# A decoder layer on one core: the output projection and the MLP with channels on the partitions, the token factor moved behind the squared ReLU

## The reference, cut to what matters

```python
merged = gates[:, :, 0] * y_attn + gates[:, :, 1] * y_pool
x = x + merged @ w_o                                  # output projection, 1024 x 1024
h2 = x * rsqrt(mean(x * x, -1) + EPS) * norm2_g       # pre-norm of the MLP, per token
u = square(relu(h2 @ w_mlp_in))                       # 1024 x 4096
x = x + u @ w_mlp_out                                 # 4096 x 1024
```

## Time and profile before

| | before |
|---|---|
| median of the runs | 1241.32 us (1241.32 to 1242.48) |
| the profiled execution | 1241.36 us, span 1239.5 us |
| PE busy | 1228.6 us, 99% of the span |
| DVE busy | 945.4 us, 76% |
| ACT busy | 563.9 us, 45% |
| POOL busy | 139.2 us, 11% |
| output projection, first matmul | 531.6 us |
| last output tile ends (the last `add_res` starts) | 625.3 us |
| down product begins (the last `up_add` of pair 15 starts) | 932.2 us |
| last matmul ends (the last add starts) | 1236.9 us |

### The profile page before, as it was taken

One profiled execution on the slowest core, in us unless ns is written; L12 is line 12 of the kernel. 1 busy time (PEld: TensorE's weight loads), 2 busy tenths in 40 slices (PEclk: granted clock), 3 DMA queues, 4 the chain that ended last, 5 costly groups with the idle time before them and its releaser, 6 DMA issues.

```text
span 1239.5 us, 16100 instructions
## 1 busy us (share of the span) xinstructions
PE 1228.6 (99%) x5822; PEld 1014.1 (82%) x5822; DVE 945.4 (76%) x1334; ACT 563.9 (45%) x971; POOL 139.2 (11%) x188
## 2 busy tenths in 40 slices
PE   8999999999999999999999999999999999999999
PEld 6878888887878888888888888888888888888887
DVE  6857876788887597845678867777769988879764
ACT  7546666665644323312345544535545333333330
POOL 1122233224100040000000000000000000000035
PEclk9999999999999999999999999999999999999999
DMA  9201211023564556422214354353479544262223
GB/s 368 78 17 35 64 40 35 19 60 95 175 235 159 184 172 221 169 86 85 102 60 162 133 173 161 129 178 139 150 263 367 210 157 152 100 237 102 102 100 138
DMA packets 111662, 173.95 MB, mean 140 GB/s; under 512 B 6240, under 2 KB 56288, under 8 KB 111584
## 3 DMA queue, kind: packets, MB, share of 16 engines
q1 hardware_dynamic: 111440, 172.92, 39.9%
q10 hardware_dynamic: 144, 0.00, 0.0%
HBM read 122.57 MB, written 50.33 MB: 139 GB/s over the span
## 4 chain that ended last, share of the span: by engine, by line
PE 88%; DVE 6%; ACT 3%; issue 2%; DMA 1%; SPq 0%; POOL 0%; ACTq 0%; DVEq 0%; POOLq 0%
PE bank L2337 79%; PE bank L2512 2%; PE bank L2467 2%; PE bank L2446 2%; PE bank L2404 1%; DMA x_tile<-in_x 1%; DVE c L2237 1%; DVE pair_lo L2131 1%; PE bank L2395 1%; DVE slot_lo L1532 1%; PE bank L2661 1%; DVE small L1622 1%; ACT prob L1102 0%; DVE gate_w_f L1882 0%; ACT slot_hi L1037 0%
## 5 line engine op out<-in xcount | busy, mean ns | idle before, releaser
L2337 PE MATMUL bank<-o_hi,s_lo 128*128 128x512 f32 (+1 forms) x452 | 175.0, 387 | 0.0
L2337 PE MATMUL bank<-o_hi,s_hi 128*128 128x512 f32 (+1 forms) x452 | 175.0, 387 | 0.0
L2237 DVE TENSOR_TENSOR c<-bank,c 128x512 f32<-128x512 f32 x112 | 75.7, 689 | 34.5 <-PE bank L2337 32.9
L2337 PE MATMUL bank<-featT_hi,pair_hi 128*128 128x512 f32 x256 | 99.8, 390 | 0.8 <-DVE c L2237 0.8
L2337 PE MATMUL bank<-o_lo,s_hi 128*128 128x512 f32 (+1 forms) x260 | 100.3, 386 | 0.0
L2337 PE MATMUL bank<-featT_lo,pair_hi 128*128 128x512 f32 x256 | 99.6, 389 | 0.0
L2337 PE MATMUL bank<-featT_hi,pair_lo 128*128 128x512 f32 x256 | 99.6, 389 | 0.0
L2337 PEld LDWEIGHTS bank<-o_hi,s_lo 128*128 128x128 f32 x452 | 84.9, 188 | 17.3
L2337 PEld LDWEIGHTS bank<-o_hi,s_hi 128*128 128x128 f32 x452 | 84.9, 188 | 17.2
L1500 ACT ACTIVATE s_hi<-s_raw 128x2048 fp32r<-128x2048 f32 x28 | 53.7, 1917 | 95.5 <-DMA s_raw<-u_store 95.5
L1476 ACT ACTIVATE c<-c 128x512 f32<-128x512 f32 x64 | 40.0, 625 | 118.9 <-DVE c L2237 118.9
(11 more groups left out here) (270 smaller groups left out, 3135.8 us busy)
## 6 DMA issues: line engine op xcount, KB each, us to landing
s_raw<-u_store SPq DMA_DIRECT2D x28, 1024.0 KB, 5.6
pair_raw<-in_w_mlp_in SPq DMA_DIRECT2D x16, 1024.0 KB, 5.7
u_store<-s_tile SPq DMA_DIRECT2D x64, 256.0 KB, 2.1
o_raw<-in_w_mlp_out SPq DMA_DIRECT2D x16, 1024.0 KB, 8.0
u_store<-u_tile SPq DMA_DIRECT2D x48, 256.0 KB, 2.3
gate_store<-out_tile SPq DMA_DIRECT2D x32, 256.0 KB, 2.1
gate_raw<-in_w_in SPq DMA_DIRECT2D x8, 1024.0 KB, 5.3
front<-in_v_and_high SPq DMA_DIRECT2D x8, 512.0 KB, 7.8
```

The lines of the kernel that those rows point to most:

```text
L2237: nc.vector.tensor_tensor(out[:], psum, other[:], ALU.add).then_inc(up_sum, 1)
L2337: mm = nc.tensor.matmul(out, a, b, start=start and i == 0, stop=stop and i == len(steps) - 1, skip_group_check=onto)
```

## The change

Output projection, up product and down product are turned: the weights are the stationary operand and the features of 512 tokens stream, so every tile has channels on its partitions and tokens along its free dimension. The numbers of matmuls of the three products stay. What follows from it:

- `h2_transpose`, `h2_norm`, `x_inverse` and the load of `g2_row` go. The gain becomes a column: ACT multiplies by it as it copies the residual (`gain`, into `z_low`, `z_high`).
- The squares of the residual are taken by ACT in place, summed over the eight channel tiles by POOL (16 copies or adds of 128 x 512), and summed over the partitions by two fp32 matmuls against ones (`token_squares`, banks 5 and 7). DVE makes the token's mean of squares from them (`token_mean`).
- The factor is left out of h2. Instead POOL multiplies the residual in `acc` by the mean (16 of 128 x 512, early in the down product), the sums gather on it, and DVE multiplies by the mean's reciprocal (`mean_inverse`, `out_scale`: 16 of 128 x 512; `scale_last_s`: the streamed operand of the last product).
- The output projection runs the high 512 tokens in its first eight tiles and the low 512 in its last eight. The sums and splits of h2 are made channel tile by channel tile, in the second half (`bottom_sum`, `difference_sums`, `fourth_sum`, `bottom_lo`, `comb_lo`, `top_lo`).
- PE runs the up products in plain order: no product of pair 1 is ahead of pair 0's. `pair_raw` has other places; the first two weight pairs are loaded after output tiles 12 and 14.
- Residual tiles are 128 x 512: 16 loads and 16 stores of 256 KB in place of 8 and 8 of 512 KB; `load_acc` likewise. The kernel writes y with channels first, and the array is turned on the host.

```diff
-            for s in range(T):
-                x_inverse(s, s, r_squared, r_mean, r_inv)
+            pool.memset(square_ones[:], 1.0).then_inc(zeroed, 1)
+            for n in range(OUTS):
+                total = square_sum[out_half(n)]
+                pool.wait_ge(squared, n + 1)
+                if n % KD == 0:
+                    pool.tensor_copy(total[:], res[n % 3][:]).then_inc(square_added, 1)
+                else:
+                    pool.wait_ge(square_added, n)
+                    pool.tensor_tensor(total[:], total[:], res[n % 3][:], ALU.add).then_inc(square_added, 1)
+
+            pool.wait_ge(mean_ready, 2)
+            for half in range(2):
+                pool.wait_ge(acc_in[half], 16 * KD)
+                for d in (4, 5, 6, 7, 0, 1, 2, 3):
+                    part = acc[:, d, HALVES[half]]
+                    pool.tensor_tensor(part, part, mean[half][:], ALU.mult).then_inc(scaled, 1)
...
+            for n in range(KD, OUTS):
+                j, second = divmod(n - KD, 2)
+                if n == OUTS - 2:
+                    for i in (P5, P4, P1):
+                        t_split_hi(0, i)
+                gain(n)
+                square(n - 1)
...
+            for k in range(4):
+                t_sum(0, k)
+            add_res(KD + 6)
+            difference_sums(3)
+            comb_lo("s4", 2)
+            for i in (P5, P4, P1):
                 t_split_lo(0, i)
-            top_split_lo(T - 1)
-            for i in (P7, P3):
-                t_split_lo(0, i)
+            top_lo(0)
+            add_res(KD + 7)
+            t_split_lo(0, P6)
+            fourth_sum(3)
+            comb_lo("s2", 3)
+            token_mean(1)
+            top_lo(1)
...
                 up_add(3, c11, p2, c11)
                 if more:
                     t_split_lo(p + 1, 5)
                     t_split_lo(p + 1, 6)
+                if p == 0:
+                    token_mean(0)
                 dve.wait_ge(p_done, turn(p, P7))
...
-                if n == D3 and t == 0:
-                    dve.wait_ge(acc_in[0], 16 * QN)
-                if n == D4 and t == 0:
-                    dve.wait_ge(acc_in[1], 16 * QN)
+                if n == D3:
+                    dve.wait_ge(scaled, t + 1)
+                if n in (D4, D5):
+                    dve.wait_ge(scaled, KD + QN * (n == D4) + t + 1)
...
+                if n == DOWN - 2:
+                    for t in range(2, QN):
+                        out_scale(t, 1, folded, 2 * QN + t + 1)
+                        out_scale(QN + t, 0, d_added, 4 * n + t + 1)
+                if n in (DOWN - 15, DOWN - 14):
+                    mean_inverse(n - DOWN + 15)
...
-            for i in range(len(LAST_PARTS)):
+            for t in range(QN):
+                out_scale(QN + t, 1, folded, 3 * QN + t + 1)
+                if t % 2 == 1:
+                    last_add(t // 2)
+            for i in range(2, len(LAST_PARTS)):
                 last_add(i)
...
                 if p == 0:
-                    pe.wait_ge(h2_lo, LEFT_READY[i])
+                    pe.wait_ge(side_lo2, LEFT_READY[i])
                 pe.wait_ge(t_ready, turn(p, i))
...
+                if p == 0 and i < 4:
+                    pe.wait_ge(res_ready, OUTS - 3 + i)
+                elif p == 0 and i == P7:
+                    pe.wait_ge(mean_ready, 1)
+                elif p == 1 and i == P5:
+                    pe.wait_ge(mean_ready, 2)
+                elif m > 7:
...
-            product(0, P5)
-            product(0, P4)
-            product(1, P5)
-            h2_transpose(T - 1)
-            product(1, P4)
             for p in range(PAIRS):
-                for i in range(0 if p > 1 else 2, 7):
+                for i in range(7):
                     product(p, i)
+                    if (p, i) == (0, P2):
+                        token_squares(0)
```

More of the change, by code:

```diff
@@ L1021, in _ @@
                 pool.tensor_tensor(p7_acc[:, t, :], p7_acc[:, t, :], shared[:, t, :], ALU.add).then_inc(folded, 1)
-                pool.tensor_tensor(acc[:, t, HALVES[1]], acc[:, t, HALVES[1]], shared[:, t, :], ALU.add).then_inc(folded, 1)
-            for i, p0 in ((D4, 0), (D5, 1)):
+                pool.tensor_tensor(acc[:, QN + t, LOW], acc[:, QN + t, LOW], shared[:, t, :], ALU.add).then_inc(folded, 1)
+            for i, first in ((D4, 0), (D5, QN)):
                 for t in range(QN):
@@ L1438, in t_split_hi, with top_hi @@
+            def top_hi(second):
+                for i in range(2):
+                    two = slice(2 * i, 2 * i + 2)
+                    if second:
+                        act.wait_ge(wo_full, OUTS)
+                    else:
+                        act.wait_ge(wo_left, 5)
+                    nc.scalar.activation(featT[0][:, QK * second + 2 * i:QK * second + 2 * i + 2, LOW], z_low[:, two, second],
+                                         ACT.Copy).then_inc(side_hi2, 1)
             def t_split_hi(p, i):
@@ L1504, in _ @@
                 if more:
-                    for i in range(2 if p == 0 else 0, 5):
+                    for i in range(5):
                         t_split_hi(p + 1, i)
@@ new lines, in token_mean, with mean_inverse @@
+            def token_mean(half):
+                dve.wait_ge(squares_full, 2 - half)
+                if half == 1:
+                    dve.wait_ge(z_ready, OUTS)
+                nc.vector.tensor_scalar(mean[half][:], bank[:, SQUARES_BANK[half], :], 1.0 / D, EPS, ALU.mult,
+                                        ALU.add).then_inc(mean_ready, 1)
+            def mean_inverse(half):
+                dve.wait_ge(scaled, 2 * KD)
+                nc.vector.reciprocal(mean[half][:], mean[half][:]).then_inc(inverse_ready, 1)
@@ L2215, in _ @@
-            for i in (P7, P3):
-                t_split_lo(0, i)
+            for n in range(KD):
+                add_res(n)
+            add_res(KD)
+            bottom_sum(0)
+            difference_sums(0)
+            add_res(KD + 1)
+            bottom_sum(1)
+            fourth_sum(0)
+            bottom_lo(0)
+            comb_lo("s3", 0)
+            comb_lo("s2", 0)
+            add_res(KD + 2)
+            bottom_sum(2)
+            difference_sums(1)
+            bottom_lo(1)
+            comb_lo("s4", 0)
@@ L2220, in _ @@
                 p5, p4, p1, p6, p2, p7, p3 = (bank[:, product_bank(p, i), :] for i in range(7))
-                if p == 0:
-                    t_sum(1, 3)
-                    for i in range(2, 5):
-                        t_split_lo(1, i)
-                elif more:
+                if more:
                     t_sums(p + 1)
@@ L2665, in _, with token_squares @@
-            for s in range(T):
-                out_projection(s, 0)
-                out_projection(s, 1, None if s == 0 else 0 if s > T - 3 else 3)
+            def token_squares(half):
+                pe.wait_ge(zeroed, 5)
+                pe.wait_ge(square_added, (OUTS, KD)[half])
+                nc.tensor.matmul(bank[:, SQUARES_BANK[half], :], square_ones[:], square_sum[half][:], start=True,
+                                 stop=True).then_inc(squares_full, 1)
+            for n in range(OUTS):
+                if n == KD + 4:
+                    token_squares(1)
+                out_projection(n)
@@ L2763 @@
         vectors.append(np.tile(np.asarray(inputs[name]).reshape(-1), 2))
+    vectors.append(np.asarray(inputs["norm2_g"]).reshape(-1))
     laid_out = {
```

465 lines of the change are left out of this document (232 added, 233 removed).

## The result

| | before | changed |
|---|---|---|
| median of the runs | 1241.76 us (1241.32 to 1242.48, 4 runs) | 1258.85 us (1258.51 to 1259.41, 4 runs) |
| ratio, 95% interval | | 1.0137 (1.012 to 1.0155) |
| the profiled execution | 1241.36 us, span 1239.5 us | 1259.41 us, span 1257.6 us |

Slower by 17.1 us; 1254 was forecast, with a range of 1243 to 1262. The page of the changed kernel, to be read beside the earlier trace rows: PE is busy 1.5 us longer, although eight groups of transposes are gone, and POOL 59 us longer.

What follows compares the result with a forecast made beforehand. PE, busy 99% of the span, was taken as the bound, so PE time and waits count: -5.5 + 8.0 (hand-over) + 6.9 (down product) + 3.0 (end) = +12.4 us, giving 1254 us, range 1243 to 1262.

Steps and rivals of the forecast that it cites:

- The sum: Whole kernel: -5.5 + 8.0 + 6.9 + 3.0 = +12.4 us on the span, giving 1254 us.
- the rival in which the clock falls: PE runs at 1.2 GHz for one product behind each of two long pauses: +5.4 us, 1259; chance 0.12.
- PE time out and in: On PE: eight transpose groups and an old pause go, two fp32 matmuls against ones come; net -5.5 us.
- The hand-over: Before the up products: PE waits +4.1 us for token_mean(0) and +3.9 for the shared SBUF port, +8.0 together.
- Product 0 starts 0.1 us late: First up product: late first weights delay DVE's low parts, so PE starts it 0.1 us late.
- Nothing covers it: the product behind it wants its bank from `up_add` 6, later still: Start of pair 1: the +4.1 us wait for token_mean(0) stays uncovered, the next product's bank being freed later still.
- The down product: POOL's 16 multiplications delay DVE through the shared port: +6.9 us of PE waiting, before products 2, 3 and 5.
- Nine turns at 1.25: Down product: seven POOL multiplications fit DVE's openings, the other nine cost DVE 1.25 us each, 11.3 us.
- The rival that DVE keeps the port: POOL gets in only at DVE's openings; down product +1.5 us, end +1, total +5.0, 1246; chance 0.18.
- The end: After PE's last matmul: DVE ends 2.4 us behind PE and stores land later; +3 us taken between 0 and 4.5.
- The reciprocals: Down product, from 1000 us on: two reciprocals on DVE, estimated at 4.3 us each, are hidden and cost nothing.
- The two rivals on the faster side: Port no obstacle to POOL: 1240, chance 0.10; DVE in time for product 7 and port free: 1237, chance 0.06.

Runs made afterwards that it cites:

- mean_moved_alone: Changed kernel with token_mean(0) placed ahead of the up sums in DVE's list, nothing else moved; 1257.17 us.
- factor_one_column: Changed kernel with POOL's 16 multiplications of the residual by the mean taking 1 of 512 columns, waits and loads kept; 1248.82 us.
- squares_one_column: Changed kernel with POOL's 14 additions to the sums of squares taking 1 of 512 columns, waits and instructions kept; 1255.15 us.
- mean_and_sums_moved: Changed kernel with token_mean(0) ahead of the up sums and, in pair 0, splits 5 and 6 behind the seventh up sum; 1252.78 us.
- factor_in_halves: Changed kernel with each of POOL's 16 multiplications of the residual done as two of 256 columns; 1250.57 us.
- factor_on_dve_late: Changed kernel with the 16 residual multiplications on DVE, the high half's eight right ahead of their additions in down products 4 and 5; 1252.21 us.
- final_scales_split: Changed kernel with four of the last twelve multiplications by the inverse factor moved from DVE to POOL; 1257.70 us.

## Why the prediction was right

- **The sum: too small by nearly a third.** The span was to grow by 12.4 us and grew by 18.1. The time lies within the range, but outside the 1249 to 1257 that got the chance of 0.52. It lies at the 1259 of the rival in which the clock falls, which got 0.12. The costs of the hand-over and of the down product are what was right. (The upper bound of 1262 was rounded up: forecast, full end and clock make +19.3, which is 1260.7; the time lies below that as well.)
- **PE time out and in: right.** -5.5 us, to 0.1.
- **The hand-over: right in size, and in its two parts.** Forecast 8.0, of which 4.1 for `token_mean(0)` late in DVE's list and 3.9 for the port; measured 7.2, and with the square sums left out 3.8 and 3.4. "Product 0 starts 0.1 us late" was wrong in the place: the port's share came out as 1.84 before product 0, 0.73 before P2 and 0.85 in the pause before pair 1. "Nothing covers it: the product behind it wants its bank from `up_add` 6, later still" is what mean_moved_alone found.
- **The down product: right in its cause, and in size partly by luck.** Forecast 6.9, measured 6.7, and all of it goes with POOL's multiplications (factor_one_column). "Nine turns at 1.25" were eleven at 1.0: both factors were off, and the products, 11.3 each, agree by luck. The waits stood before products 3 and 5, where 2, 3 and 5 were named. The rival that DVE keeps the port falls with the first long instruction behind another (948.33, 3.37 us).
- **The clock: the step that was left out of the sum.** The rival "the clock falls in the pauses" is the forecast with this term added, and it is what happened: +3.3 us, not the 5.4 of one whole product behind each of two pauses. That its 1259 meets the time is luck: 1.3 us more at the end and the 2.1 of the start make up for its smaller size and for waits that came out 1.0 shorter. The same sum forecast a pause of 4 us and 6.9 us of waiting in pieces, so 0.12 was too little for it; the sum should have carried it. The Trainium skill (TensorE: Matmul & The Clock Gate, What's actually happening) has the clock fall after an idle window. The trace agrees behind the waits of 4.66 and 4.91 us; behind shorter ones the runs show either outcome (last section).
- **The end: mis-sized.** +3 was a value between 0 and 4.5; it measured +4.3, almost the 4.5 that the stores alone give. DVE, which was to end 2.4 us behind PE, ended 1.3 behind it.
- **The reciprocals: nothing, as forecast.** They took 3.35 us each, less than the estimate of 4.3, and PE waits for nothing there.
- **The first 20 us: not in the forecast, +2.1,** and by the other profiles with six ones most likely chance; no run shows it.

With clock and end at their measured values and the rest as it was the forecast would have been 1258.4. The two rivals on the faster side are out: the port is an obstacle (squares_one_column, factor_one_column), and DVE was not in time for product 7 (the pause of 4.66 us).

## What to carry to other kernels

An engine that is 99% full in the kernel before loses nearly every wait that a change makes, so look at the place of each new instruction in the other engines' lists, and not only at their load: three instructions moved in DVE's list gave 6.1 us back. If GpSimd must work beside a full VectorE, give it short pieces: here the same work in halves cost PE 1.3 us of waiting and not 6.7. And when a forecast contains a pause of several us on TensorE, put slow matmuls behind it into the sum.

## What the runs showed of the hardware

- Between 945 and 1000 us GpSimd got a turn between two VectorE instructions that both read SBUF twice, and VectorE paid once for each such pair: about 1.0 us beside POOL pieces of 512 columns, 0.5 beside 256 (eleven pairs in each kernel). An instruction that follows two PSUM readers paid 0.0 to 0.1.
- TensorE's fall to 1.2 GHz does not have to begin right behind the pause. After a wait of 1.83 us (mean_and_sums_moved) five matmuls ran at the usual 0.23 us behind the first, and the next ones 0.4 apart; PE's timeline:

```profile
622.09 0.47 PE L2459 MATMUL bank<-featT_hi,pair_hi 128*128 128x512 f32 x1 [1.83 <-DVE comb_lo L2148]
622.39 0.39 PE L2459 MATMUL bank<-featT_hi,pair_lo 128*128 128x512 f32 x1
...
623.53 0.59 PE L2459 MATMUL bank<-featT_hi,pair_hi 128*128 128x512 f32 x1
623.92 0.63 PE L2459 MATMUL bank<-featT_hi,pair_lo 128*128 128x512 f32 x1
624.34 0.63 PE L2459 MATMUL bank<-featT_lo,pair_hi 128*128 128x512 f32 x1
```

  There the wait before P2 was gone, taken up by the slower pace.
- The same wait can be followed by either pace. Nine of the profiles have the wait of 1.83 to 1.84 us before product 0; matmuls at the slow level follow it in four (mean_and_sums_moved, factor_in_halves, factor_on_dve_late, final_scales_split) and not in the five others. The pause at the kernel's start, 1.48 to 1.87 us, and the wait of 2.05 us before product 7 have both outcomes too. What decides stays open.
- The profile's granted clock does not show every such stretch: in the first 14 us it reads 1.00 in all profiles, with matmuls 0.43 us apart in seven of them. The trace of the changed kernel has its first record of the clock only at 12.1 us, where the pace rises.
